# Merge and output projection of a two-block model in pairs of slabs, seven block products for eight, with the sums of weights on GpSimd

## The chip, the cores and the metric

The kernel runs on one core of one Trainium2 chip. The metric is the time of one execution on the device in microseconds (us), the median of the runs shown. All arithmetic spoken of here is fp32.

## What is computed

Two transformer-like blocks follow each other on a sequence of 512 tokens of width 1024. The first has differential attention, a state-space layer and a mixture of 32 experts. The second, of which the change touches the last part, is cut here to what matters:

```python
proj = h @ w_in                       # q, k, v, x_rnn, z_rnn, z_attn, g_r, g_a
y_rnn  = (hr * silu(z_rnn)) @ w_out_rnn
y_attn = (o * silu(z_attn)) @ w_out_attn
merged = sigmoid(g_r + b_r) * y_rnn + sigmoid(g_a + b_a) * y_attn
x = x + gate * (merged @ w_o)
return rms_norm(x, g_final)
```

g_r and g_a are two 1024x1024 products of h, y_rnn and y_attn one each of the gated recurrent output (`rnn_out`) and the gated attention output (`attn_out`), and the last one of `merged`: five products of 1024x1024 weights with 1024x512 activations.

## The kernel before

Every engine has a program of its own, and the programs meet at semaphores: the order on each engine is written out by hand. Activations are kept transposed, features on the 128 partitions and the 512 tokens along the free dimension, as tiles [128, 8, 512] (`h_t`, `rnn_out`, `attn_out`, `merged`, `x_t`). A weight matrix is cut into slabs: slab i holds the weights of 128 output features, [128, 8 k-tiles, 128]. One slab takes eight matmuls of 512 columns, added up in one PSUM bank. In the trace each fp32 matmul stands as two MATMUL records, and each record has its weight load (LDWEIGHTS) beside it.

The heads. Before the part in question, a loop over eight heads (`HEADS2`) runs, on TensorE, five slabs of a head (`turn_slab`, L1089: q, k, x_rnn, z_rnn, z_attn), the scores (L1116), the gates of the recurrence (L1119), the transposes of the softmax (L1124) and the product with v (L1137). ScalarE copies and squashes (L1504 to L1525; the transposed softmax is copied by L1274). VectorE rotates (L2116 to L2118), convolves (L2123, L2125), normalizes the softmax (L2139), does the recurrence (L2144 to L2152; the last of these counts `rnn gated`) and makes `attn_out` (L2157, counts `head gated`). GpSimd has nothing to do here.

The merge. In the last head the slot in which the next head's first slab would run is filled by `merge_slab(0, 0)`, after a wait for the first of four ScalarE copies. Then come the other 31 slabs (L1096), for i in 0..7 the four kinds g_r, o_r, g_a, o_a in PSUM banks 0 to 3. ScalarE makes the sigmoids from banks 0 and 2 (L1534), VectorE multiplies them with banks 1 and 3 (L2164) and adds the two into `merged` (L2166).

The output. Eight slabs of w_o (L1159) go into banks 4 to 7. VectorE adds each, times the gate, to x (L2169), ScalarE squares it (L1537), VectorE adds squares up (L2175), TensorE sums them over the partitions (`square_sum`, L805), ScalarE takes the root (L1539), and after a reciprocal (L2177) and four transposes (L1168) VectorE scales the output (L2181), which SyncE stores.

Loads. SyncE loads the merge slabs (512 KB each) into ring slots 5 to 8 and the w_o slabs into slots 0 to 3, each after a wait for the slab before it in its slot; turn slabs are in slots 0 to 4.

Of the kernel before, what the change touches and what calls it, by code (L numbers as in the profile page):

```python
# [11 lines left out]
ACT = mybir.ActivationFunctionType  # L12
# [73 lines left out]
MASKED = -1e30  # L86
PI = float(np.pi)
# [23 lines left out]
def program(nc, io):  # L111


    with ExitStack() as ctx:
# [182 lines left out]
        sig_r, sig_a = work[:, 0, :], work[:, 1, :]  # L297
# [26 lines left out]
        def sync_engine():  # L324
# [154 lines left out]
            for s in range(4):  # L479
                load_slab("merge", 5 + s, s)  # L480
# [13 lines left out]
            for s in range(4):  # L494
                if s < 2:
                    swap_halves(HEADS2 - 1, s)
                sp.wait_ge(sem("turn slabs used"), 5 * (HEADS2 - 1) + s + 1)
                load_slab("o", s, s)
            for i in range(1, KT):
                for s in range(4):  # L500
                    sp.wait_ge(sem("merge slabs used"), 4 * (i - 1) + s + 1)
                    load_slab("merge", 5 + s, 4 * i + s)
            for s in range(4):
                sp.wait_ge(sem("o slabs used"), s + 1)
                load_slab("o", s, 4 + s)
# [8 lines left out]
        def tensor_engine():  # L514
# [76 lines left out]
            pe.wait_ge(sem("ready for idle products"), 1)  # L591
# [4 lines left out]
            pe.wait_ge(sem("c_act"), 1)  # L596
# [47 lines left out]
            def s5_output(q):  # L644

                pe.wait_ge(sem("s5 states"), q + 1)
                if q:
                    pe.wait_ge(sem("s5 y read"), q)
                else:
                    pe.wait_ge(sem("s5 direct kept"), 1)  # L650
# [12 lines left out]
            def scores_of(i):  # L663
                q_h, k_h = proj[:, 4 + i, :], proj[:, 8 + i, :]
                pe.wait_ge(sem("pair kept"), kept[("slab", 5 + 3 * i)])
                if i:
                    pe.wait_ge(sem("p turned kept"), 4 * i)
                    pe.wait_ge(sem("masked"), 8 * i)
                else:
                    pe.wait_ge(sem("s5 direct kept"), 1)  # L670
                    pe.wait_ge(sem("s5 sums kept"), 8)
# [420 lines left out]
            def merge_slab(i, s):  # L1092

                pe.wait_ge(sem(f"slot {5 + s} loaded"), 16 * (i + 1) + (32 if s == 3 else 16 * 2 * (9 - ROWS_TO)))
# [5 lines left out]
            pe.wait_ge(sem("second tables loaded"), 32)  # L1100
            for i in range(HEADS2):
# [39 lines left out]
            pe.wait_ge(sem("rnn gated"), 8)  # L1141
            for i in range(KT):
                for s in range(4):
                    if (i, s) == (0, 0):
                        continue
                    if (i, s) == (0, 3):
                        pe.wait_ge(sem("head gated"), 8)
                    if i:
                        pe.wait_ge(sem("merge gate sig" if s % 2 == 0 else "merge gated"), 2 * (i - 1) + s // 2 + 1)
                    merge_slab(i, s)  # L1150
            for i in range(2):
                for s in range(4):
                    pe.wait_ge(sem(f"slot {s} loaded"), 16 * (15 + i))
                    if i:
                        pe.wait_ge(sem("x mixed"), 8 + s + 1)
                    for k in range(KT):
                        if (i, s) == (0, 0):
                            pe.wait_ge(sem("merged"), k + 1)
                        mm = pe.matmul(psum[:, 4 + s, :], ring[:, s, k, :], merged[:, k, :], start=(k == 0), stop=(k == KT - 1))  # L1159
                    mm.then_inc(sem("o slabs used"), 1)  # L1160

            pe.wait_ge(sem("squares added"), 12)
            square_sum(0, True, False)
            pe.wait_ge(sem("norm squares"), 24)
            square_sum(7, False, True).then_inc(sem("norm sum"), 1)
# [6 lines left out]
        def scalar_engine():  # L1172
# [133 lines left out]
            act.activation(flat[:, 4096:4608], psum[:, 4, :], ACT.Copy).then_inc(sem("s5 direct kept"), 1)  # L1306
# [162 lines left out]
            act.dma_start(pos_i, io["positions"]).then_inc(sem("second tables loaded"), 16)  # L1469
            act.dma_start(arena[:, low:low + 2048], io["rnn_gates"]).then_inc(sem("second tables loaded"), 16)  # L1470
# [23 lines left out]
            for i in range(HEADS2):  # L1494
# [22 lines left out]
                act.activation(tanh_g, r_g, ACT.Tanh, scale=all_par[:, 7, i:i + 1]).then_inc(sem("tanh made"), 1)  # L1517
                act.wait_ge(sem("tanh made"), i + 1)
# [9 lines left out]
            act.wait_ge(sem("head gated"), 8)  # L1528
            for i in range(KT):
                for n in range(2):  # L1530
                    act.wait_ge(sem("merge slabs used"), 4 * i + 2 * n + 1)
                    if i:
                        act.wait_ge(sem("merged"), i)
                    act.activation((sig_r, sig_a)[n], psum[:, 2 * n, :], ACT.Sigmoid, bias=gates_par[:, n, i:i + 1]).then_inc(sem("merge gate sig"), 1)  # L1534
            for k in range(KT):
                act.wait_ge(sem("x mixed"), 8 + k + 1)
                act.activation(h_t[:, k, :], x_t[:, k, :], ACT.Square).then_inc(sem("norm squares"), 1)  # L1537
            act.wait_ge(sem("norm sum"), 3)
            act.activation(last_std, psum[:, 1, 0:TT], ACT.Sqrt, bias=const("eps"), scale=1.0 / D).then_inc(sem("norm root"), 1)  # L1539


        def vector_engine():
# [11 lines left out]
            dve.memset(proj[:, 0, 0:2 * P], 0.0).then_inc(sem("ready for idle products"), 1)  # L1554
# [538 lines left out]
            dve.wait_ge(sem("second tables loaded"), 32)  # L2093
# [19 lines left out]
            for i in range(HEADS2):  # L2113
# [27 lines left out]
                dve.wait_ge(sem("a made"), i + 1)  # L2141
# [18 lines left out]
            for i in range(KT):  # L2160
                for n, sig in enumerate((sig_r, sig_a)):
                    dve.wait_ge(sem("merge slabs used"), 4 * i + 2 * n + 2)
                    dve.wait_ge(sem("merge gate sig"), 2 * i + n + 1)
                    dve.tensor_tensor(sig, sig, psum[:, 2 * n + 1, :], ALU.mult).then_inc(sem("merge gated"), 1)  # L2164
                dve.wait_ge(sem("merge gated"), 2 * i + 2)
                dve.tensor_tensor(merged[:, i, :], sig_r, sig_a, ALU.add).then_inc(sem("merged"), 1)  # L2166
            for k in range(KT):
                dve.wait_ge(sem("o slabs used"), k + 1)
                dve.scalar_tensor_tensor(x_t[:, k, :], psum[:, 4 + k % 4, :], mods[:, 64 + k:65 + k], x_t[:, k, :], ALU.mult, ALU.add).then_inc(sem("x mixed"), 1)  # L2169

                for n in {2: (1,), 3: (2,), 4: (3,), 5: (4,), 6: (5, 6)}.get(k, ()):
                    dve.wait_ge(sem("norm squares"), 16 + n + 1)
                    if n > 1:
                        dve.wait_ge(sem("squares added"), 6 + n - 1)
                    dve.tensor_tensor(h_t[:, 0, :], h_t[:, 0, :], h_t[:, n, :], ALU.add).then_inc(sem("squares added"), 1)  # L2175
# [3 lines left out]
            dve.wait_ge(sem("x mixed"), 16)  # L2179
# [4 lines left out]
        def gpsimd_engine():  # L2184
# [36 lines left out]
            for n in range(TT * TOPK):  # L2221
                pool.indirect_dma_start(out=parts[:, n, :], out_offset=None, in_=y_rows, in_offset=bass.IndirectOffsetOnAxis(ap=slot_i[:, n:n + 1], axis=0)
                                        ).then_inc(sem(f"parts {n // TOPK} gathered" if n >= TOPK else f"first parts {n} gathered"), 16)

# [87 lines left out]
def layout(a):  # L2312
# [23 lines left out]
    for part, (bb, cc) in enumerate(((a["ssm_b_re"], a["ssm_c_re"]), (a["ssm_b_im"], a["ssm_c_im"]))):  # L2336
# [23 lines left out]
        "merge_slabs": np.stack([g_r, o_r, g_a, o_a], 1).reshape(4 * KT, P, D),  # L2360
        "v_slabs": v, "o_slabs": o_o,
# [21 lines left out]
```

## Time and profile before

| | us |
|---|---|
| median of 3 runs | 2064.86 |
| lowest and highest run | 2064.61, 2068.92 |
| span of the profiled execution, first to last instruction | 2063.5 |

The profiled execution's own time is not listed apart; what it has beside the span is taken as the difference to the median, 1.4 us. In the profile PE is TensorE's matmuls, PEld its weight loads, DVE VectorE, ACT ScalarE, POOL GpSimd, SP SyncE. A row of a timeline has the start, the duration, the engine, the line, the operation with what it writes and reads, the count of merged instructions, and in brackets the idle time before it with what ended that. Since matmuls are pipelined and their ends are modelled, a stretch of PE is best read from the start of one row to the start of the next.

### The profile page before, as it was taken

The page shows a single profiled execution, that of the slowest core. Times are in us where ns is not written, and L with a number is a line of the kernel's source. Part 1 is how long each engine was busy: PE and PEld are TensorE (multiplying, and loading weights), DVE is VectorE, ACT ScalarE, POOL GpSimd, SP SyncE. Part 2 cuts the span into 40 slices and gives each one's busy share as a digit, 9 for nine tenths or more (in the row PEclk, how much of TensorE's full clock was granted, in tenths as well). Part 3 has the DMA queues.
Part 4 walks back from the last instruction along what each step waited for, and adds up shares of the span by engine and source line. Part 5 has one row for each costly group of instructions (what it writes and reads, how often), then busy time and mean ns, then how long its engine had stood idle before and what let it go on. Part 6 is the DMA issues. An engine that isn't in the chain of part 4 may idle for free.

```text
span 2063.5 us, 35675 instructions
## 1 busy us (share of the span) xinstructions
PE 1999.2 (97%) x15505; PEld 894.2 (43%) x15505; DVE 660.3 (32%) x1287; ACT 404.5 (20%) x837; POOL 52.8 (3%) x54
## 2 busy tenths in 40 slices
PE   8999998999999999999999999889999999999998
PEld 4455543334434434344333343455444444444443
DVE  5979864111111112121111121153434453300002
ACT  3224412111101101011011010112333533300001
POOL 0000000000000000000000000030000000000000
PEclk9999999999999999999999999989999999999999
DMA  8474788999899999999999999870312221122211
GB/s 328 142 289 182 304 289 343 420 419 361 327 421 419 420 420 419 419 420 420 420 419 419 418 418 420 343 265 15 111 65 74 64 65 65 53 80 74 80 33 69
DMA packets 109166, 553.77 MB, mean 268 GB/s; under 512 B 14864, under 2 KB 26128, under 8 KB 59216
## 3 DMA queue, kind: packets, MB, share of 16 engines
q1 hardware_dynamic: 87232, 517.23, 62.5%
q10 hardware_dynamic: 14720, 17.43, 2.5%
q0 software_dynamic: 7056, 16.79, 2.2%
q8 instruction: 125, 2.05, 0.4%
q14 instruction: 33, 0.27, 0.0%
HBM read 532.91 MB, written 26.35 MB: 271 GB/s over the span
## 4 chain that ended last, share of the span: by engine, by line
PE 69%; DMA 13%; SPq 13%; DVE 2%; issue 1%; ACT 1%; POOL 0%; ACTq 0%; POOLq 0%; DVEq 0%
PE psum L904 16%; PE psum L1089 13%; SPq L435 12%; PE psum L1096 11%; DMA arena<-in_w 7%; PE psum L912 7%; PE psum L575 7%; DMA ring<-in_w 3%; PE psum L1047 3%; PE psum L1159 3%; DMA arena<-in_mod_slabs 1%; PE psum L1137 1%; PE psum L1116 1%; PE psum L897 1%; PE psum L884 1%
## 5 line engine op out<-in xcount | busy, mean ns | idle before, releaser
L904 PE MATMUL psum<-arena,ring 128*32 128x512 f32 x4096 | 452.1, 595 | 12.4 <-DMA arena<-in_w 11.8
L1089 PE MATMUL psum<-h_t,ring 128*128 128x512 f32 x640 | 278.6, 593 | 0.2 <-ACT arena L1462 0.2
L904 PEld LDWEIGHTS psum<-arena,ring 128*32 128x32 f32 x4096 | 134.0, 110 | 310.8 <-issue 308.2
L912 PE MATMUL psum<-arena,h_t 128*32 128x256 f32 x3840 | 217.8, 380 | 4.0 <-DMA arena<-in_w 3.1
L1988 DVE TENSOR_SCALAR h_t<-psum 128x512 f32<-128x512 f32 (+2 forms) x33 | 27.9, 845 | 577.2 <-PE psum L904 577.2
L1390 ACT ACTIVATE ring<-psum,mods,gain 128x64 f32<-128x64 f32 (+2 forms) x264 | 85.6, 428 | 613.0 <-PE psum L884 613.0
L1089 PEld LDWEIGHTS psum<-h_t,ring 128*128 128x128 f32 x640 | 120.6, 190 | 146.2 <-issue 145.7
L912 PEld LDWEIGHTS psum<-arena,h_t 128*32 128x32 f32 x3840 | 121.0, 110 | 100.4 <-issue 18.7
L904 PE MATMUL psum<-ring 128*32 128x512 f32 x1344 | 148.8, 593 | 5.5 <-DMA ring<-in_w 5.4
L575 PE MATMUL psum<-h_t,ring 128*128 128x512 f32 x256 | 117.1, 613 | 2.6 <-ACT h_t L1210 2.6
L1096 PE MATMUL psum<-h_t,ring 128*128 128x512 f32 x256 | 112.6, 593 | 1.4 <-ACT work L1274 1.4
L1096 PE MATMUL psum<-arena,ring 128*128 128x512 f32 x256 | 112.5, 593 | 0.0
L912 PE MATMUL psum<-ring,h_t 128*32 128x256 f32 x1600 | 90.5, 380 | 3.2 <-DMA ring<-in_w 3.2
L904 PEld LDWEIGHTS psum<-ring 128*32 128x32 f32 x1344 | 44.4, 110 | 103.5 <-issue 103.5
L2002 DVE COPY h_t<-psum 128x512 f32<-128x512 f32 (+2 forms) x33 | 27.9, 845 | 154.9 <-PE psum L920 154.9
L575 PEld LDWEIGHTS psum<-h_t,ring 128*128 128x128 f32 x256 | 48.8, 196 | 63.7 <-issue 62.8
L1096 PEld LDWEIGHTS psum<-h_t,ring 128*128 128x128 f32 x256 | 48.6, 190 | 62.3 <-issue 60.7
L1096 PEld LDWEIGHTS psum<-arena,ring 128*128 128x128 f32 x256 | 48.6, 190 | 60.7 <-issue 60.7
L2164 DVE TENSOR_TENSOR work<-work,psum 128x512 f32<-128x512 f32 x16 | 11.0, 689 | 196.7 <-PE psum L1096 196.7
L1398 ACT ACTIVATE work<-psum 128x512 f32<-128x512 f32 (+2 forms) x33 | 23.8, 720 | 239.4 <-PE psum L912 239.4
L912 PEld LDWEIGHTS psum<-ring,h_t 128*32 128x32 f32 x1600 | 50.0, 110 | 42.9 <-issue 6.9
L2190 POOL DMA_INDIRECT ring<-h_rows,row_i x33 | 35.6, 1080 | 1143.5 <-PE psum L884 836.7
(440 smaller groups left out, 1748.9 us busy)
## 6 DMA issues: line engine op xcount, KB each, us to landing
arena<-in_w SPq DMA_DIRECT2D x288, 1024.0 KB, 27.8
ring<-in_w SPq DMA_DIRECT2D x96, 1024.0 KB, 29.2
ring<-in_dot_slabs SPq DMA_DIRECT2D x40, 512.0 KB, 5.6
ring<-in_turn_slabs SPq DMA_DIRECT2D x40, 512.0 KB, 3.4
ring<-in_merge_slabs SPq DMA_DIRECT2D x32, 512.0 KB, 3.3
ring<-in_mod_slabs SPq DMA_DIRECT2D x6, 2048.0 KB, 10.8
ring<-in_proj_slabs SPq DMA_DIRECT2D x24, 512.0 KB, 4.1
y_rows<-arena SPq DMA_DIRECT2D x3, 3584.0 KB, 25.4
```

What stands on the lines that cost most here:

```text
L435: sp.dma_start(slot[s], source).then_inc(sem(f"weights {s} loaded"), 16)
L575: mm = pe.matmul(bank, ring[:, n % 4, k, :], src[:, k, :], start=(k == 0), stop=(k == KT - 1))
L904: mm = pe.matmul(psum[32 * j:32 * j + 32, g, :], x_e[:, c * tokens + g * TG:c * tokens + g * TG + TG], slot[s][:, j * S:(j + 1) * S], star ...
L912: mm = pe.matmul(psum[32 * j:32 * j + 32, 6 + g // 2, (g % 2) * 256:(g % 2) * 256 + 256], h_e[:, g * 256 + half * P + 32 * c:g * 256 + hal ...
L1047: mm = pe.matmul(psum[:, 4 + i, :], h_t[:, k, t * P:(t + 1) * P], ring[:, 4 * i + 4:4 * i + 8, k, :], start=(k == 0), stop=(k == KT - 1))
L1089: mm = pe.matmul(psum[:, bank, :], ring[:, s, k, :], h_t[:, k, :], start=(k == 0), stop=(k == KT - 1))
L1096: mm = pe.matmul(psum[:, s, :], ring[:, 5 + s, k, :], (h_t, rnn_out, h_t, attn_out)[s][:, k, :], start=(k == 0), stop=(k == KT - 1))
L1159: mm = pe.matmul(psum[:, 4 + s, :], ring[:, s, k, :], merged[:, k, :], start=(k == 0), stop=(k == KT - 1))
L1390: act.activation(x_e[:, k * tokens:(k + 1) * tokens], psum[:, 4 + k // 4, (k % 4) * tokens:(k % 4 + 1) * tokens], ACT.Identity, bias=mods[ ...
L1988: dve.tensor_scalar(gate, psum[:, 0:groups, 0:256], LIMIT, None, ALU.min).then_inc(sem("gate clipped"), 1)
L2002: dve.tensor_copy(h_e[:, 0:256 * groups], src[:, 0:256 * groups]).then_inc(sem("h_e kept"), 1)
L2190: pool.indirect_dma_start(out=x_g[n][0:rows, :], out_offset=None, in_=h_rows, in_offset=bass.IndirectOffsetOnAxis(ap=index, axis=0), bound ...
```

## The change

The 32 merge slabs and 8 output slabs are taken in pairs, in the order of `MERGE_PAIRS`: for j in 0..3 the pairs (g_r, g_a, o_r, o_a), then four pairs of w_o; 20 in all. A pair is a product of a 256x1024 matrix with 1024x512 activations. Weights are halved along the output features (`first`, `second` slab) and along the input features (k-tiles 0:4 and 4:8), activations along the input features and the tokens (`front`, `back`, 256 each). Seven block products of four matmuls with 256 columns then take the place of eight, in Winograd's arrangement of Strassen's scheme, with eight sums of operands and seven of results:

- GpSimd makes four sums of activations for each source (`moving_sums`: h, rnn_out, attn_out with four operations of [128, 4, 256], merged in two parts) and four sums of weights for each pair (`slab_sums`: four operations of [128, 4, 128], one of them in place). `slab_sums(n)` waits for the load of pair n and for the end of pair n-2, whose buffers it takes. In GpSimd's program the sums of rnn_out and attn_out stand behind `slab_sums(1)` and ahead of `slab_sums(2)`.
- ScalarE copies the first product (`keep_p1`), makes sigmoids in quarters of the pair, and squares in quarters.
- VectorE makes `u2`, `u4` and three blocks (256 columns each) for a pair, then the gating (`y gated`, `merged`) and, for the last two slabs of merged, the sums of activations (`last merged sums`).
- The five additions of squares move from VectorE to GpSimd.
- SyncE loads 20 pairs of 1 MB into ring slots 5-6, 7-8 and 0-1, pair n after the end of pair n-3.
- Some semaphores are merged into others, their waits renumbered.

TensorE, cut to its core:

```diff
-            def merge_slab(i, s):
-                pe.wait_ge(sem(f"slot {5 + s} loaded"), ...)
-                for k in range(KT):
-                    mm = pe.matmul(psum[:, s, :], ring[:, 5 + s, k, :], (h_t, rnn_out, h_t, attn_out)[s][:, k, :], start=(k == 0), stop=(k == KT - 1))
-                mm.then_inc(sem("merge slabs used"), 1)
+            def product(out, stationary, moving, start=False):
+                for k in range(4):
+                    mm = pe.matmul(out, stationary[:, k, :], moving[:, k, :], start=(start and k == 0), stop=(k == 3), skip_group_check=True)
+                mm.then_inc(sem("products"), 1)
+
+            def pair_begun(n):
...
+                product(block_x, first[:, 0:4, :], moving[:, 0:4, front], True)
+                pe.wait_ge(sem("slab sums"), 4 * n + 2)
+                if n:
+                    pe.wait_ge(sem("pair steps"), 5 * (n - 1) + U2)
+                if (kind, j) == ("o", 0):
+                    pe.wait_ge(sem("moving sums"), 16)
+                    pe.wait_ge(sem("last merged sums"), 2)
+                product(block_x2, mixed[:, 1, :, :], t2, True)
+                pe.wait_ge(sem("x bank kept"), P1_KEPT(n))
+                if (kind, j) == ("o", 0):
+                    pe.wait_ge(sem("merged"), 8)
+                product(block_x, first[:, 4:8, :], moving[:, 4:8, front])
+                if n:
+                    pe.wait_ge(sem("pair steps"), 5 * (n - 1) + U4)
+                else:
+                    pe.wait_ge(sem("p turned kept"), 16 + 4 * HEADS2)
+                product(block_v, mixed[:, 0, :, :], t1, True)
+
+            def pair_ended(n):
...
+                product(block_q, second[:, 0:4, :], t3, True)
+                pe.wait_ge(sem("slab sums"), 4 * n + 4)
+                if n:
+                    pe.wait_ge(sem("pair steps"), 5 * (n - 1) + BLOCK_12)
+                product(block_w, mixed[:, 2, :, :], moving[:, 4:8, back], True)
+                pe.wait_ge(sem("pair steps"), 5 * n + BLOCK_22)
+                if (kind, j) == ("o", 0):
+                    pe.wait_ge(sem("last merged sums"), 3)
+                product(block_q, second[:, 4:8, :], t4)
...
-                    pe.wait_ge(sem("p turned kept"), 16 + 4 * i + 1)
-                    merge_slab(0, 0)
+                    pe.wait_ge(sem("rnn gate sig"), 2 * i + 2)
+                    pair_begun(0)
```

GpSimd and VectorE:

```diff
+            def slab_sums(n):
+                at = PAIR_AT[n % 3]
+                first, second, (s1, s2, s4) = ring[:, at, :, :], ring[:, at + 1, :, :], (sums_of[n % 2][:, a, :, :] for a in range(3))
+                pool.wait_ge(sem(f"slot {PAIR_AT[n % 3]} loaded"), PAIR_LOADED[n % 3] + 16 * (n // 3 + 1))
+                if n >= 2:
+                    pool.wait_ge(sem("products"), 7 * (n - 2) + 7)
+                else:
+                    pool.wait_ge(sem("turn slabs used"), 5 * (HEADS2 - 1) + 4 + n)
+                pool.tensor_tensor(s1, second[:, 0:4, :], second[:, 4:8, :], ALU.add).then_inc(sem("slab sums"), 1)
+                pool.wait_ge(sem("slab sums"), 4 * n + 1)
+                pool.tensor_tensor(s2, s1, first[:, 0:4, :], ALU.subtract).then_inc(sem("slab sums"), 1)
+                pool.tensor_tensor(second[:, 0:4, :], first[:, 0:4, :], second[:, 0:4, :], ALU.subtract).then_inc(sem("slab sums"), 1)
+                pool.wait_ge(sem("slab sums"), 4 * n + 2)
+                pool.tensor_tensor(s4, first[:, 4:8, :], s2, ALU.subtract).then_inc(sem("slab sums"), 1)
+
+            moving_sums(0, h_t, h_sums)
+            slab_sums(0)
+            slab_sums(1)
+            pool.wait_ge(sem("rnn gated"), 8)
+            moving_sums(4, rnn_out, rnn_sums)
+            pool.wait_ge(sem("head gated"), 8)
+            moving_sums(8, attn_out, attn_sums)
+            for n in range(2, 16):
+                slab_sums(n)
...
+            def u2_of(n):
+                dve.wait_ge(sem("products"), 7 * n + 2)
+                dve.wait_ge(sem("x bank kept"), P1_KEPT(n))
+                dve.tensor_tensor(u2, block_x2, p1_kept, ALU.add).then_inc(sem("pair steps"), 1)
+
+            def u4_of(n):
+                dve.wait_ge(sem("products"), 7 * n + 4)
+                dve.wait_ge(sem("pair steps"), 5 * n + U2)
+                dve.tensor_tensor(u4, block_v, u2, ALU.add).then_inc(sem("pair steps"), 1)
+                dve.wait_ge(sem("pair steps"), 5 * n + U4)
+
+            def block(n, products, out, bank, u):
+                dve.wait_ge(sem("products"), 7 * n + products)
+                dve.tensor_tensor(out, bank, u, ALU.add).then_inc(sem("pair steps"), 1)
```

## Rows read from the trace of the kernel before

**Rows 1.** The page's head: span, busy time of each engine, clock granted to TensorE.

```profile
span 2063.5 us, 35675 instructions
...
PE 1999.2 (97%) x15505; PEld 894.2 (43%) x15505; DVE 660.3 (32%) x1287; ACT 404.5 (20%) x837; POOL 52.8 (3%) x54
...
PEclk9999999999999999999999999989999999999999
```

**Rows 2.** Windows: the merge, the output slabs, the tail (busy us of each engine).

```profile
1783.40:1996.30 212.90, 212.90 (x499) 94.38 (x498) 15.86 (x23) 10.99 (x16) 0.00 (x0) 1.00 0.20 68
1996.30:2051.20 54.90, 54.90 (x129) 24.32 (x128) 10.32 (x15) 4.42 (x7) 0.00 (x0) 1.00 0.11 39
2051.20:2063.50 12.30, 3.13 (x21) 2.54 (x19) 6.28 (x10) 2.18 (x3) 0.00 (x0) 0.61 0.46 171
```

**Rows 3.** Timeline of PE: end of the last head, first and last merge slabs.

```profile
1760.90 2.32 PE L1116 MATMUL psum<-arena 128*128 128x128 f32 x8
1763.06 1.88 PE L1119 MATMUL psum<-arena 128*128 128x512 f32 x4
...
1771.65 1.26 PE L1124 MATMUL psum<-consts,work 128*128 128x128 f32 x10
1774.28 7.13 PE L1096 MATMUL psum<-h_t,ring 128*128 128x512 f32 x16 [1.38 <-ACT work L1274]
1781.25 2.32 PE L1137 MATMUL psum<-work,arena 128*128 128x512 f32 x8
1783.40 7.03 PE L1096 MATMUL psum<-arena,ring 128*128 128x512 f32 x16
1790.28 7.03 PE L1096 MATMUL psum<-h_t,ring 128*128 128x512 f32 x16
...
1989.41 7.03 PE L1096 MATMUL psum<-arena,ring 128*128 128x512 f32 x16
1996.27 55.10 PE L1159 MATMUL psum<-arena,ring 128*128 128x512 f32 x128
```

**Rows 4.** Timeline of PEld in the tail: eight weight loads for one-column matmuls.

```profile
2052.87 0.97 PEld L805 LDWEIGHTS psum<-consts,h_t 128*128 128x128 f32 x8 [0.81 <-ACT h_t L1537]
```

**Rows 5.** Timeline of ACT at the end of the last head.

```profile
1773.65 1.40 ACT L1274 ACTIVATE work<-psum 128x512 f32<-128x512 f32 x4
1775.06 1.28 ACT L1525 ACT_TABLE_LOAD   x1
1776.36 0.60 ACT L1525 ACTIVATE arena<-psum 128x512 f32<-128x512 f32 x1
```

**Rows 6.** Groups by line and form: DVE and ACT with 256 columns (mean ns).

```profile
L1774 DVE CUSTOM_DVE_ANT_0 work<-psum,consts 128x256 f32<-128x256 f32 x8 | 3.4, 420 | 0.0
L1274 ACT ACTIVATE work<-psum 128x256 f32<-128x256 f32 x8 | 3.1, 383 | 0.0
```

**Rows 7.** Timeline of DVE at the end of the last head.

```profile
1773.78 0.69 DVE L2144 TENSOR_TENSOR arena<-arena 128x512 f32<-128x512 f32 x1 [5.66 <-ACT arena L1520]
...
1779.39 0.69 DVE L2152 TENSOR_TENSOR arena<-arena 128x512 f32<-128x512 f32 x1
...
1783.68 0.69 DVE L2157 TENSOR_TENSOR arena<-psum,arena 128x512 f32<-128x512 f32 x1 [3.00 <-PE psum L1137]
```

**Rows 8.** Groups by line and form of POOL: its one operation on much data.

```profile
L2186 POOL MEMSET arena<- 128x1024 f32 x1 | 1.0, 952 | 48.8 <-PE psum L551 48.8
```

**Rows 9.** The chain that ended last, from the last output slab on.

```profile
1996.44 54.95 PE psum L1159 x128
...
2051.41 0.76 DVE x_t L2169
...
2052.19 0.63 ACT h_t L1537
```

**Rows 10.** DMA issues: KB each, median us from issue to landing.

```profile
ring<-in_merge_slabs SPq DMA_DIRECT2D x32, 512.0 KB, 3.3
ring<-in_mod_slabs SPq DMA_DIRECT2D x6, 2048.0 KB, 10.8
```

More of the change, by code:

```diff
@@ L86 @@
 MASKED = -1e30
+HALF = S // 2
+MERGE_PAIRS = [(kind, j) for j in range(KT // 2) for kind in ("g_r", "g_a", "o_r", "o_a")] + [("o", j) for j in range(KT // 2)]
 PI = float(np.pi)
@@ L493, in sync_engine @@
                     load_slab("turn", s, 5 * i + s)
[L494 to L505, printed above, removed]
+            for s in range(2):
+                swap_halves(HEADS2 - 1, s)
+            sp.wait_ge(sem("turn slabs used"), 5 * (HEADS2 - 1) + 2)
+            load_pair(2)
+            for n in range(3, len(MERGE_PAIRS)):
+                sp.wait_ge(sem("products"), 7 * (n - 3) + 7)
+                load_pair(n)
             for k in range(KT):
@@ L588, in keep_on @@
                     pe.matmul(psum[:, bank, :], identity, dilated, start=True, stop=True, skip_group_check=True)
-            pe.wait_ge(sem("ready for idle products"), 1)
+            pe.wait_ge(sem("c_act"), 1)
             for _ in range(14):
@@ L595, in tensor_engine @@
             rms_sum(0, h_t)
[L596 removed]
+            pe.wait_ge(sem("c_act"), 2)
             mod_row(0, 0)
@@ L1099, in tensor_engine @@
             pe.wait_ge(sem("v rows kept"), 8)
-            pe.wait_ge(sem("second tables loaded"), 32)
+            pe.wait_ge(sem("late tables loaded"), 64)
             for i in range(HEADS2):
@@ L1138, in tensor_engine, with token_squares @@
                 mm.then_inc(sem("head out"), 1)
[L1141 to L1165, printed above, removed]
+            pair_ended(0)
+            for n in range(1, len(MERGE_PAIRS)):
+                pair_begun(n)
+                pair_ended(n)
+            def token_squares(k, tiles, first=False, last=False):
+                for t in tiles:
+                    mm = pe.matmul(psum[:, 6, t:t + 1], h_t[:, k, t * P:(t + 1) * P], ones[:, 0:1], start=(first and t == 0), stop=last, skip_group_check=True)
+                return mm
+            pe.wait_ge(sem("squares added"), 6 + 5)
+            token_squares(0, range(TT), first=True)
+            pe.wait_ge(sem("norm squares"), 16 + 4 * 4 - 1)
+            token_squares(6, range(TT))
+            token_squares(7, (2, 3), last=True)
+            pe.wait_ge(sem("norm squares"), 16 + 4 * 4)
+            token_squares(7, (0, 1), last=True).then_inc(sem("norm sum"), 1)
             pe.wait_ge(sem("tile scale"), TT + 2)
@@ L1525, in scalar_engine @@
                 act.activation(za_s, psum[:, 6, :], ACT.Sigmoid).then_inc(sem("z_attn sig"), 1)
[L1528 to L1534, printed above, removed]
@@ L1551, in scaled @@
                     dve.scalar_tensor_tensor(h_t[:, k, :], x_t[:, k, :], gain[:, k:k + 1], rstd, ALU.mult, ALU.mult).then_inc(sem("h scaled"), 1)
-            dve.memset(proj[:, 0, 0:2 * P], 0.0).then_inc(sem("ready for idle products"), 1)
+            dve.memset(proj[:, 0, 0:2 * P], 0.0).then_inc(sem("c_act"), 1)
             dve.wait_ge(sem("sines"), 1)
@@ L2157, in vector_engine @@
                 dve.tensor_tensor(attn_out[:, i, :], psum[:, 7, :], za_s, ALU.mult).then_inc(sem("head gated"), 1)
[L2160 to L2166, printed above, removed]
@@ new lines, in mixed @@
+            def mixed(k, part, y):
+                dve.scalar_tensor_tensor(x_t[:, k, part], y, mods[:, 64 + k:65 + k], x_t[:, k, part], ALU.mult, ALU.add).then_inc(sem("x mixed"), 1)
+            for n, (kind, j) in enumerate(MERGE_PAIRS):
+                if kind != "o":
+                    continue
+                u2_of(n)
+                dve.wait_ge(sem("products"), 7 * n + 3)
+                dve.scalar_tensor_tensor(x_t[:, 2 * j, front], block_x, mods[:, 64 + 2 * j:65 + 2 * j], x_t[:, 2 * j, front], ALU.mult, ALU.add).then_inc(sem("x mixed"), 1)
+                u4_of(n)
+                for step_made, products, i, part, bank, u in ((BLOCK_22, 5, 1, back, block_q, u4), (BLOCK_12, 6, 0, back, block_w, u4), (BLOCK_21, 7, 1, front, block_q, u2)):
+                    block(n, products, y_pair[:, i, part], bank, u)
+                    dve.wait_ge(sem("pair steps"), 5 * n + step_made)
+                    mixed(2 * j + i, part, y_pair[:, i, part])
@@ new lines, in gpsimd_engine @@
+            pool.wait_ge(sem("h ready"), 8 + KT * TT)
+            pool.wait_ge(sem("v product"), 8)
+            moving_sums(0, h_t, h_sums)
[7 more added lines that the diff above has]
+                slab_sums(n)
+            t1, t2, t3, t4 = h_sums
+            pool.wait_ge(sem("products"), 7 * 14)
@@ new lines, in gpsimd_engine @@
+            pool.tensor_tensor(t4[:, 0:2, :], merged[:, 4:6, front], t2[:, 0:2, :], ALU.subtract).then_inc(sem("moving sums"), 1)
+            for n in range(16, len(MERGE_PAIRS)):
+                slab_sums(n)
+            for n, (k, squares_made) in enumerate(((1, 4), (2, 8), (3, 8), (4, 12), (5, 12))):
+                pool.wait_ge(sem("norm squares"), 16 + squares_made)
+                if n:
+                    pool.wait_ge(sem("squares added"), 6 + n)
+                pool.tensor_tensor(h_t[:, 0, :], h_t[:, 0, :], h_t[:, k, :], ALU.add).then_inc(sem("squares added"), 1)
```

167 lines of the change are left out of this document (139 added, 28 removed).

## The prediction

> **What bounds the kernel now.** I read the page's head first: PE is busy 97% of 2063.5 us at full clock, every other engine a third or less [rows 1]. The windows then show the stretch that is changed: 212.9 us of merge and 54.9 us of output slabs, in which PE is busy all the time, DVE at most 19%, ACT 8%, POOL not at all [rows 2]. So here PE's own work is the time, and what shortens it counts in full as long as nothing new makes PE wait. The timeline of PE gives the unit: slabs start at 1783.40, 1790.28, and the last at 1989.41, the output slabs at 1996.27: (1996.27 - 1783.40) / 31 = 6.867 us for a slab, and a first output matmul that waited for nothing [rows 3]. A pair of slabs costs 13.73 us. The chain that ended last goes from the last slab through DVE and ACT to the end, so a gain on PE moves the whole tail forward [rows 9].
>
> **The change, part by part.**
>
> 1. *Seven products for eight.* A pair becomes 7 x 4 = 28 matmuls of 256 columns, 56 records. A record of 512 columns takes 6.867 / 16 = 0.4292 us. To cost one of 256 I need the fixed part. L1137 and L1116 each run eight records of 512, 384, 256 and 128 columns (two each, 2560 in all) and take 1783.40 - 1781.25 = 2.15 and 1763.06 - 1760.90 = 2.16 us [rows 3]. With a + b x columns, the first gives b = 0.836 ns, a = 1.4 ns, the second b = 0.829 and a = 4.7. A record of 256 columns is then 0.2153 to 0.2170 us; I take 0.216. A pair costs 56 x 0.216 = 12.10 us and saves 1.63 us (1.58 to 1.67). Weight loads could set the pace now that a record is half as long, but eight of them with matmuls of one column took 0.97 us, 0.12 each, well under 0.216 [rows 4].
>
> 2. *The waits between products.* There are now 140 seams on PE with up to four waits each instead of 40 with two. L1137 ends in records of 128 columns, and the slab behind it, with two waits ahead of it (its load and `rnn gated`), starts without a gap in the 2.15 us above [rows 3]. I take a met wait at nothing; the cover is the record that runs meanwhile. Below nothing it can't go, since the waits are added. The other end I leave to a rival.
>
> 3. *The first pair.* `merge_slab(0, 0)` waited 1.38 us for ACT's copy; `pair_begun(0)` waits for gates that were ready earlier and starts right behind the transposes, at 1771.65 + 10 x 0.109 = 1772.74. P1 and P2 take 1.73 each, to 1776.2. P3 waits for `keep_p1`, which stands on ACT behind the sigmoid that ends at 1776.96 [rows 5] and takes 0.38 [rows 6]: P3 starts at 1777.4, P4 ends at 1780.85, the product with v at 1783.0, against 1783.40. P5 to P7 end at 1788.2. DVE is in time for P7's wait (P7 would start at 1786.5): `attn_out` from 1783.3 to 1784.0 [rows 7], then u2, u4 and the first block at 0.42 each [rows 6], the last behind P5: 1785.4. Before, two slabs ended at 1790.28. Gain 2.1 us. The other 19 pairs give 19 x 1.63 = 31.0.
>
> 4. *DVE and ACT inside a pair.* Five steps of 0.42 and, for o pairs, two to four of 0.69 [rows 6, 7] make at most 4.9 us of DVE in 12.1; ACT has at most five of about 0.4 to 0.5. Each PE wait on them has a product (1.73 us) or more between the work and its use: keeping P1 (0.38) beside P2, block 22 (0.42) beside P6. Hidden, at nothing. If a step came 1.3 us late, it would show as that excess times 20.
>
> 5. *Entering the output product.* Before, no gap [rows 3]. Now, with T the end of pair 15, DVE has from T - 1.5 on one block (0.42), the gating, merged, and two sums of 0.72 each: ready at T + 1.8; P2 of pair 16 wants it at T + 1.73. The front half follows at T + 3.75, for P3 at T + 3.5. Loss 0.3 us.
>
> 6. *Loads.* 1 MB per pair, issued when pair n-3 ends, so 12.1 us before GpSimd may begin on it. 512 KB landed in 3.3 us, 2048 KB in 10.8 [rows 10]: 1 MB within 11, hidden. SP's other work, the swaps of the last head, keeps its place ahead of load 2.
>
> 7. *GpSimd's sums.* The trace has no such operation. The nearest POOL row is a memset of 1024 columns, 0.952 us, so 0.48 us for 512, with one stream [rows 8]; DVE's addition of 512 takes 0.69 [rows 7]. A sum has three streams, two in and one out. Taking the memset's rate for each gives t = 3 x 0.48 = 1.43 us per 512 columns. I take that; ends are 0.48 (one stream) and twice 1.43, 2.9. Four per pair are 5.7 us against 12.1, hidden in the steady state. The tight place is pair 2: behind `slab_sums(1)` stand the sums of rnn_out and attn_out, and then S1 and S2 of pair 2. `rnn gated` comes at 1780.1 [rows 7]; from there on the queue holds 8 operations of 1024 columns and 2 of 512, 18 t. PE wants S2 after P1 of pair 2, at 1788.2 + 12.1 + 1.73 = 1802.0. The slack is 21.9 us, used up at t = 1.22. With 1.43 it is 18 x 1.43 = 25.7 plus some 0.3 of handing over: PE stands 4.1 us. Behind it GpSimd catches up, since 5.7 is less than 12.1. The sums of h (8 t) come in the first head, seven heads before their use; those of merged begin at the end of pair 13 and have 25 us for 9 t.
> The Trainium skill, "GPSIMD Engine Reference", section 3.1, states 4497 ns for an addition of 2048 columns. That would be t = 1.12 (an estimate from that page), with no stall at pair 2 and a time 4.1 us lower than my sum; no row here shows it.
>
> 8. *Tail.* Instead of L2169 and the square (0.76 and 0.63 us [rows 9]) three steps of 0.42 with 256 columns follow the last product: 0.1 us less. The additions of squares on GpSimd end a pair earlier than needed.
>
> Sum against the profiled execution: 2063.5 - 2.1 - 31.0 + 0.3 + 4.1 - 0.1 = 2034.7 us. The median of the runs lies 1.4 us over that span, so I expect 2036.0.
>
> **The rivals.**
>
> *All hidden.* t is under 1.22, so pair 2 does not wait: 4.1 less, 2031.9. For it: the memset's rate leaves room for 2.5 streams in 1.22 us. Against: three streams.
>
> *GpSimd and VectorE hold each other up.* If the two can't read two operands each at once, whoever comes second waits a whole operation. It bites where both have such work. In the last head, DVE's recurrence (eight operations from 1773.78 on [rows 7]) meets `slab_sums(1)`, begun at 1771.8: the third DVE operation starts at 1778.9 and not 1775.2, so `rnn gated`, and pair 2 with it, comes 3.7 us later. At the entry of the output product `slab_sums(17)` begins at T, and between DVE's five operations stand three or four of 1.43: merged is ready at T + 8.9 for 3.75, 5.2 lost. Together 8.9: 2045; with t = 1.2 the same working gives 2.8 + 4.2, on top of no stall otherwise: 2039. Before, POOL ran nothing in these stretches [rows 2], so the rows say nothing for or against. The Trainium skill, "SBUF — State Buffer", section "Who interferes with whom", says that a VectorE instruction with two SBUF inputs and a GpSimd one that reads SBUF share a read interface and block each other for the whole instruction; by that rule this rival holds. No row here shows it.
>
> *The seams on PE cost.* A wait costs 0.1 us at each of 140 products: 14 us, 2050. Against it, the seam behind L1137.
>
> *Slower: GpSimd becomes the bound.* With t over 3.03, four sums outlast the 12.1 us of a pair. With t = 3.5: 18 x 3.5 - 21.9 = 41 at pair 2, and 17 x (14 - 12.1) = 32 behind it, less the 33 gained: 2105. It decides from t = 3.05, where pair 2 alone eats 33 us. It takes six memsets' time for one sum; little speaks for that.
>
> That the scheme doesn't shorten PE (matmuls of 256 columns at the price of 512) is excluded by the 2.15 us of L1137.
>
> **How the numbers follow.** Forecast, a stall of 2 to 7 us at pair 2, 2033 to 2039: 0.40. All hidden: 0.22, near 2031.9. Holding up, 2039 to 2046: 0.22. Seams, 2040 to 2050: 0.07. t from 1.7 to 3, 2041 to 2064: 0.06. Slower: 0.03. The range 2031.0 to 2047.0 holds the first three and part of the others. 0.2% is about 4 us, what a measurement of this kernel tells from no change; all cases but t near 3 and the slower one lie beyond: faster 0.95, same 0.02, slower 0.03.
>
> **What would show it.** In the new timeline, PE's P1 of consecutive pairs 12.1 us apart; records of 256 columns 0.216 apart; one gap of some 4 us ahead of P2 of pair 2, released by POOL; POOL sums of 512 columns near 1.43 us; DVE's recurrence in the last head still 0.69 each with 0.03 between (holding up shows as gaps or long operations beside POOL's); a gap under 0.5 us around P2 and P3 of pair 16. Gaps at most products would make the seams right; P2 waiting for POOL in every pair, GpSimd as bound.

## The result and the profile after

The changed kernel takes 2040.13 us (median of 4 runs, 2039.04 to 2041.46) against 2065.30 of the kernel before in the same runs: a ratio of 0.9868, 95% interval 0.9854 to 0.9882. That is 25.2 us less; 28.8 were forecast. The profiled run took 2039.04 us, 1.3 us more than its span of 2037.7.

The page's head, as in [rows 1], and its groups of the new products and sums:

```profile
span 2037.7 us, 37038 instructions
...
PE 1973.6 (97%) x15993; PEld 991.7 (49%) x15993; DVE 718.6 (35%) x1392; ACT 421.9 (21%) x889; POOL 199.3 (10%) x155
...
L1117 PE MATMUL psum<-arena,ring 128*128 128x256 f32 x544 | 120.5, 380 | 1.6 <-POOL ring L2386 1.4
...
L2384 POOL TENSOR_TENSOR ring<-ring 128x512 f32<-128x512 f32 x20 | 25.3, 1267 | 416.7 <-PE psum L1112 314.9
```

PE is 25.6 us less busy, POOL 146 us more. The waits of PE at the new products (L1117) are a short list (the view of the waits: who waits, for whom, total, times, longest):

```profile
PE psum L1117 <- DVE ring L2297: 2.0, 1, 2.0
PE psum L1117 <- ACT work L1604: 1.8, 1, 1.8
PE psum L1117 <- POOL ring L2386: 1.4, 1, 1.4
```

Three single waits, none that comes back with each pair. The timeline of PE shows where they stand (as [rows 3]):

```profile
1772.58 1.26 PE L1203 MATMUL psum<-consts,work 128*128 128x128 f32 x10
1773.67 1.89 PE L1117 MATMUL psum<-h_t,ring 128*128 128x256 f32 x8
1775.40 1.89 PE L1117 MATMUL psum<-ring 128*128 128x256 f32 x8
1779.04 1.99 PE L1117 MATMUL psum<-h_t,ring 128*128 128x256 f32 x8 [1.76 <-ACT work L1604]
...
1789.94 1.89 PE L1117 MATMUL psum<-h_t,ring 128*128 128x256 f32 x8
1791.66 1.89 PE L1117 MATMUL psum<-ring 128*128 128x256 f32 x8
...
1802.03 1.89 PE L1117 MATMUL psum<-arena,ring 128*128 128x256 f32 x8
1805.33 22.71 PE L1117 MATMUL psum<-arena,ring 128*128 128x256 f32 x104 [1.42 <-POOL ring L2386]
...
1976.86 3.22 PE L1117 MATMUL psum<-ring 128*128 128x256 f32 x8 [2.04 <-DVE ring L2297]
1980.21 2.27 PE L1117 MATMUL psum<-arena,ring 128*128 128x256 f32 x8
1982.32 3.62 PE L1117 MATMUL psum<-ring 128*128 128x256 f32 x16
...
2025.48 2.73 PE L1228 MATMUL psum<-consts,h_t 128*128 128x1 f32 x24
```

The first product of pair 1 starts at 1789.94, that of pair 2 at 1802.03: a pair takes 12.09 us. A product of eight records takes 1.727 us from start to start (1791.66 - 1789.94), 0.216 a record, and seven of them make the whole 12.09: nothing is left for the waits between them.

The part ahead of the last head isn't touched but for small edits, and from one profiled run to another it ends up to 8.5 us apart (the transposes start between 1769.3 and 1777.8). So I read every profile from the start of the last head's transposes (L1203; L1124 before) to the end of the span. Before, that is 2063.5 - 1771.65 = 291.85 us, after 2037.7 - 1772.58 = 265.1: 26.7 us gained, and 0.9 lost ahead of it. That 0.9 lies inside the 8.5 us by which this point moves, and I did not look further.

| us, from the transposes on | forecast | measured |
|---|---|---|
| pair 0 | 2.1 less | 1.3 less (1789.94 - 1772.58 against 1790.28 - 1771.65) |
| 19 pairs | 31.0 less | 31.2 less (19 x (13.73 - 12.09)) |
| gap at pair 2 | 4.1 more | 1.6 more (second product at 1805.33, due at 1791.66 + 12.09) |
| entry of pair 16 | 0.3 more | 4.3 more (fourth product at 1982.32, due 1805.33 + 3.45 + 14 x 12.09 = 1978.04) |
| tail | 0.1 less | 0.1 less (2037.7 - 2025.48 against 2063.5 - 2051.21) |
| sum | 28.8 less | 26.7 less |

The large term is right to 1%. The small ones are off in both directions, and the timelines of DVE and POOL say why. First the recurrence in the last head (as [rows 7]) and what POOL does beside it:

```profile
1775.53 1.76 DVE L2239 TENSOR_TENSOR arena<-arena 128x512 f32<-128x512 f32 x1 [5.66 <-ACT arena L1592]
1777.32 1.63 DVE L2240 SCALAR_TENSOR_TENSOR arena<-arena 128x512 f32<-128x512 f32 x1
1778.99 0.69 DVE L2241 TENSOR_TENSOR arena<-arena 128x512 f32<-128x512 f32 x1
...
1783.16 0.69 DVE L2247 TENSOR_TENSOR arena<-arena 128x512 f32<-128x512 f32 x1
```

```profile
1774.24 1.28 POOL L2386 TENSOR_TENSOR ring<-ring 128x512 f32<-128x512 f32 x1
1775.47 1.28 POOL L2387 TENSOR_TENSOR ring<-ring 128x512 f32<-128x512 f32 x1
1776.70 1.71 POOL L2389 TENSOR_TENSOR ring<-ring 128x512 f32<-128x512 f32 x1
1783.93 2.36 POOL L2369 TENSOR_TENSOR arena<-arena 128x1024 f32<-128x1024 f32 x1 [5.52 <-DVE arena L2247]
```

The second operation of the recurrence in the kernel before, with the first one in [rows 7]:

```profile
1774.50 0.69 DVE L2145 SCALAR_TENSOR_TENSOR arena<-arena 128x512 f32<-128x512 f32 x1
```

As long as POOL works, the first two DVE operations take 1.76 and 1.63 us where they took 0.69, and those after it is done take 0.69; POOL's last one takes 1.71 instead of 1.28. The recurrence lasts 8.3 us from the first start to the end of L2247 where it lasted 6.3. The same at the entry of pair 16, DVE and POOL:

```profile
1972.58 0.69 DVE L2290 TENSOR_TENSOR arena<-work 128x512 f32<-128x512 f32 x1
1973.31 1.74 DVE L2296 TENSOR_TENSOR ring<-arena,ring 128x512 f32<-128x512 f32 x1
1974.97 1.75 DVE L2297 TENSOR_TENSOR ring<-arena 128x512 f32<-128x512 f32 x1
1976.64 0.41 DVE L2268 TENSOR_TENSOR arena<-psum,work 128x256 f32<-128x256 f32 x1
1977.08 1.31 DVE L2287 TENSOR_TENSOR work<-work,arena 128x512 f32<-128x512 f32 x1
1978.42 1.64 DVE L2290 TENSOR_TENSOR arena<-work 128x512 f32<-128x512 f32 x1
```

```profile
1973.23 1.26 POOL L2384 TENSOR_TENSOR ring<-ring 128x512 f32<-128x512 f32 x1 [6.69 <-PE psum L1117]
...
1977.80 1.71 POOL L2389 TENSOR_TENSOR ring<-ring 128x512 f32<-128x512 f32 x1
```

L2268, with one input in PSUM and one in SBUF, keeps its 0.41 us in the midst of it; four operations with both inputs in SBUF are held up (1.31 to 1.75 us for 0.69). The end of L2290 at 1980.06 is the earliest at which the third product can start.

### The profile page after: what moved, and what is told of

It is laid out like the page before. It is cut to its first block, busy times and chain, and to the rows that moved or that the text cites. A ratio compares the mean times of both kernels' runs of the same rounds, so it can differ in the third digit from the quotient of the medians.

```text
span 2037.7 us, 37038 instructions
## 1 busy us (share of the span) xinstructions
PE 1973.6 (97%) x15993; PEld 991.7 (49%) x15993; DVE 718.6 (35%) x1392; ACT 421.9 (21%) x889; POOL 199.3 (10%) x155
## 3 DMA queue, kind: packets, MB, share of 16 engines
q8 instruction: 129, 2.11, 0.4%
## 4 chain that ended last, share of the span: by engine, by line
PE 69%; SPq 14%; DMA 10%; DVE 3%; issue 1%; POOL 1%; ACT 1%; ACTq 0%; POOLq 0%; DVEq 0%
PE psum L927 17%; SPq L458 14%; PE psum L1112 13%; PE psum L1117 11%; PE psum L935 8%; PE psum L598 7%; DMA ring<-in_w 5%; DMA arena<-in_w 3%; PE psum L1070 3%; DMA arena<-in_mod_slabs 1%; PE psum L920 1%; PE psum L1195 1%; PE psum L1216 1%; PE psum L907 1%; PE psum L782 1%
## 5 line engine op out<-in xcount | busy, mean ns | idle before, releaser
L1112 PE MATMUL psum<-h_t,ring 128*128 128x512 f32 x640 | 278.6, 592 | 0.2 <-ACT arena L1534 0.2
L1112 PEld LDWEIGHTS psum<-h_t,ring 128*128 128x128 f32 x640 | 120.4, 190 | 146.4 <-issue 145.9
L1117 PE MATMUL psum<-arena,ring 128*128 128x256 f32 x544 | 120.5, 380 | 1.6 <-POOL ring L2386 1.4
L598 PE MATMUL psum<-h_t,ring 128*128 128x512 f32 x256 | 116.3, 609 | 2.6 <-ACT h_t L1282 2.6
L1117 PEld LDWEIGHTS psum<-arena,ring 128*128 128x128 f32 x544 | 103.4, 191 | 16.7 <-POOL ring L2386 1.8
L598 PEld LDWEIGHTS psum<-h_t,ring 128*128 128x128 f32 x256 | 48.4, 194 | 62.4 <-issue 61.3
L1117 PE MATMUL psum<-ring 128*128 128x256 f32 x288 | 67.6, 384 | 2.0 <-DVE ring L2297 2.0
L2384 POOL TENSOR_TENSOR ring<-ring 128x512 f32<-128x512 f32 x20 | 25.3, 1267 | 416.7 <-PE psum L1112 314.9
L1117 PEld LDWEIGHTS psum<-ring 128*128 128x128 f32 x288 | 55.2, 192 | 10.0 <-POOL ring L2386 2.4
```

Source lines behind the costliest of these rows:

```text
L598: mm = pe.matmul(bank, ring[:, n % 4, k, :], src[:, k, :], start=(k == 0), stop=(k == KT - 1))
L1112: mm = pe.matmul(psum[:, bank, :], ring[:, s, k, :], h_t[:, k, :], start=(k == 0), stop=(k == KT - 1))
L1117: mm = pe.matmul(out, stationary[:, k, :], moving[:, k, :], start=(start and k == 0), stop=(k == 3), skip_group_check=True)
L2384: pool.tensor_tensor(s1, second[:, 0:4, :], second[:, 4:8, :], ALU.add).then_inc(sem("slab sums"), 1)
```

## The experiments

Two theories. A: GpSimd and VectorE block each other where both read two operands from SBUF, and this is what lies behind the gap at pair 16, the late recurrence and part of the other two gaps. B: the gaps are the length of the chains on VectorE and of GpSimd's queue, and the slow operations only coincide with them.

The 95% intervals of the ratios of e2, e3 and e5 overlap that of the changed kernel (0.9854 to 0.9882, repeated 0.9842 to 0.9894). Their gains are therefore read from the profiles, one profiled execution each, over the stretch from the transposes on; there the changed kernel repeats to 0.1 us (e6).

**e1_small_sums.** GpSimd's sums are made on one column only, in `moving_sums`, `slab_sums` and the sums of merged.

```diff
+            def tiny(out, one, two, op):
+                return pool.tensor_tensor(out[:, 0, 0:1], one[:, 0, 0:1], two[:, 0, 0:1], op)
...
-                pool.tensor_tensor(s1, second[:, 0:4, :], second[:, 4:8, :], ALU.add).then_inc(sem("slab sums"), 1)
+                tiny(s1, second[:, 0:4, :], second[:, 4:8, :], ALU.add).then_inc(sem("slab sums"), 1)
```

> Every sum on GpSimd is done on one column only, with the same waits and counts, so GpSimd takes almost no time and the output is not the reference's (the sums of weights and activations are left out). Theory A (GpSimd and VectorE block each other when both read two operands from SBUF, and the stall at pair 2 is GpSimd's queue): the VectorE operations of the recurrence in the last head go back from 1.7 to 0.69 us, the 1.4 us gap ahead of the second product of pair 2 goes, and at the entry of pair 16 the 2.0 us gap and the slow matmuls behind it go: 5.1 us less than the changed kernel, near 2035. Theory B (the waits lie in the order of the work on VectorE and in PE's seams, GpSimd only happens to run beside it): the gap at pair 2 goes, 1.4 us less, the VectorE operations stay at 1.7 us and pair 16 keeps its gap. Both: the 1.8 us wait for ScalarE's copy in the last head stays.

Measured: 2033.16 us, ratio 0.9834 (0.9821 to 0.9847) to the kernel before. The recurrence runs at 0.69 again, the gaps at pairs 2 and 16 are gone, and from the transposes on it takes 258.8 us, 6.3 less than the changed kernel. The sums of weights and activations are left out in this kernel, so it is no candidate, only a measure. Its list of waits holds one of the three, and smaller than expected:

```profile
PE psum L1117 <- ACT work L1604: 0.9, 1, 0.9
```

That was a miss of both theories as I had put them (1.8 was expected to stay): part of this wait hangs on GpSimd too. The last run, e8, shows how.

**e2_hold_17.**

```diff
             for n in range(16, len(MERGE_PAIRS)):
+                if n == 17:
+                    pool.wait_ge(sem("last merged sums"), 3)
                 slab_sums(n)
```

> GpSimd waits with the sums of pair 17 until VectorE has made its last sums of merged, so that nothing runs on GpSimd beside VectorE's gating at the entry of pair 16. Theory A: VectorE's five operations there take 0.69 each again, PE's gap of 2.0 us shrinks to under 0.4, no half clock follows (1.6 us of it in the second product of pair 16 and 0.4 in the third), together 3.5 to 4 us less than the changed kernel: near 2036.5. Theory B: the gap stays as it is, since the chain on VectorE is what it is. The last head and pair 2 stay as in the changed kernel.

Measured: 2035.62 us, ratio 0.9851 (0.9837 to 0.9864). From the transposes on 261.1 us, 4.0 less than the changed kernel, all of it at pair 16. DVE and PE there:

```profile
1973.48 0.69 DVE L2296 TENSOR_TENSOR ring<-arena,ring 128x512 f32<-128x512 f32 x1
1974.09 0.69 DVE L2297 TENSOR_TENSOR ring<-arena 128x512 f32<-128x512 f32 x1
...
1975.87 0.69 DVE L2290 TENSOR_TENSOR arena<-work 128x512 f32<-128x512 f32 x1
```

```profile
1974.93 1.97 PE L1117 MATMUL psum<-ring 128*128 128x256 f32 x8
1976.73 1.95 PE L1117 MATMUL psum<-arena,ring 128*128 128x256 f32 x8
1978.51 3.62 PE L1117 MATMUL psum<-ring 128*128 128x256 f32 x16
```

The second product starts at 1974.93, the fourth 3.58 later, where 3.45 is the undisturbed spacing: with 0.1 us ahead of the second product some 0.2 us are left, near the 0.3 that the prediction gave this place. Theory B falls at pair 16; the chain on VectorE is short enough when nothing runs on GpSimd beside it.

**e3_apart.**

```diff
             slab_sums(0)
-            slab_sums(1)
             pool.wait_ge(sem("rnn gated"), 8)
+            slab_sums(1)
             moving_sums(4, rnn_out, rnn_sums)
+            slab_sums(2)
             pool.wait_ge(sem("head gated"), 8)
             moving_sums(8, attn_out, attn_sums)
-            for n in range(2, 16):
+            for n in range(3, 16):
                 slab_sums(n)
```

> GpSimd waits for the end of VectorE's recurrence in the last head before it makes the sums of pair 1, and makes the sums of pair 2 ahead of those of attn_out. Theory A: the recurrence's first two operations go from 1.76 and 1.63 to 0.69, so that it ends 2.0 us earlier, near 1781.2 against 1783.2; the gap of 1.4 us at pair 2 goes, none comes at pair 1 (its sum is needed at 1791.7 and ready near 1784) nor at pair 3; 1.4 us less than the changed kernel, near 2038.7, the gap at pair 16 stays. Theory B: the recurrence stays as long as it was.

Measured: 2035.74 us, ratio 0.9849 (0.9836 to 0.9863); from the transposes on 262.7, 2.4 less than the changed kernel. All six plain operations of the recurrence take 0.69 us and no gap stands at pairs 1 to 3. The gain is 1 us beyond the expectation; the last section says where it comes from.

**e5_order.** `slab_sums(1)` stays beside the recurrence.

```diff
             moving_sums(4, rnn_out, rnn_sums)
+            slab_sums(2)
             pool.wait_ge(sem("head gated"), 8)
             moving_sums(8, attn_out, attn_sums)
-            for n in range(2, 16):
+            for n in range(3, 16):
```

> Only the order of GpSimd's work is changed: the sums of pair 2 stand ahead of the sums of attn_out, the sums of pair 1 still run beside VectorE's recurrence. If the gap at pair 2 is the length of GpSimd's queue alone, it goes (1.6 us less than the changed kernel, near 2038.5), while the recurrence's two slow operations of 1.7 us stay: blocking there costs nothing once the queue has room. If the late recurrence reaches PE in another way (through attn_out or block 22 of pair 0), a gap shows in pair 0 or at pair 3.

Measured: 2034.40 us, ratio 0.9855 (0.9827 to 0.9883; its runs scatter from 2027.75 to 2039.92). From the transposes on 262.7, the same as e3_apart. The recurrence has its 1.74 and 1.63 us, the gap at pair 2 is gone and none has come for it. So a late recurrence costs nothing by itself; it cost 1.6 us because the queue ahead of pair 2 had no room to spare.

**e6_changed_again.** The changed kernel without an edit.

> The changed kernel once more, beside the other runs of this call: near 2040, with 1.8 us ahead of the third product, 1.4 at pair 2, 2.0 at pair 16 and a pair in 12.09 us. It tells how far the time of one kernel moves between calls; every theory expects the same.

Measured: 2037.47 us, ratio 0.9868 (0.9842 to 0.9894), the same ratio as at first. From the transposes on 265.2 (265.1 at first), with gaps of 1.8, 1.4 and 2.05 us. The two profiled spans differ by 1.5 us (2037.7 and 2036.2), all of it ahead of that stretch; the medians differ by 2.7.

**e4_ten_sums.** Each of the first two sums of weights four times.

```diff
+                for _ in range(3):
+                    step(pool, pool.tensor_tensor(s1, second[:, 0:4, :], second[:, 4:8, :], ALU.add), "more sums")
                 pool.tensor_tensor(s1, second[:, 0:4, :], second[:, 4:8, :], ALU.add).then_inc(sem("slab sums"), 1)
```

> The first two sums of weights of each pair are made four times each, ten operations in place of four. If GpSimd's work is hidden as long as it is shorter than a pair (both theories) its ten operations take about 12.9 us beside a pair of 12.1: PE waits some 0.8 us in each pair behind pair 2, 14 us in all, the queue ahead of pair 2 grows by some 12 us and the sums of merged put another 6 on the path ahead of pair 16: 2065 to 2075, no gain over the kernel before. If the sums were already in PE's way in every pair, it would be 20 x 7.9 = 158 us more.

Measured: 2084.71 us, ratio 1.0084 (1.0068 to 1.0099): slower than before, by more than expected, and far from 158 us. PE's waits from the second block on:

```profile
PE psum L1117 <- POOL ring L2390: 35.9, 15, 11.5
PE psum L1117 <- DVE work L2268: 3.7, 1, 3.7
PE psum L1117 <- ACT work L1604: 1.2, 1, 1.2
```

The 11.5 us are pair 2, as computed from the queue; 9.1 of the other 24.4 stand at pair 16, where 6 were expected. The expectation missed two things. The ten operations take 13.1 us a pair even where nothing holds them up (1853.43 to 1866.51), not 12.9: each added one waits for the one before, 1.35 us from start to start and not 1.23. Beside VectorE they take up to 14.7 (1838.75 to 1853.43, single ones 1.60 to 1.72 for 1.27). And VectorE's recurrence is now blocked eight times, so that attn_out and block 22 of pair 0 come late (3.7). The slower side is there once GpSimd's work outlasts the 12.09 us of a pair, here by 1 us and more; where exactly it begins no run shows.

**e7_all_mended.** e3_apart and e2_hold_17 together, and ScalarE's copy of the first product of pair 0 ahead of the last sigmoid:

```diff
                 keep_turned(4 + i + 1, pt2)
+                if i == HEADS2 - 1:
+                    act.wait_ge(sem("products"), 1)
+                    act.activation(p1_kept, block_x, ACT.Copy).then_inc(sem("x bank kept"), 1)
...
             for n, (kind, j) in enumerate(MERGE_PAIRS):
-                keep_p1(n)
+                if n:
+                    keep_p1(n)
```

> Four edits together: GpSimd's sums of pair 1 behind the recurrence, those of pair 2 ahead of attn_out's, those of pair 17 behind VectorE's last sums of merged, and ScalarE's copy of the first product of pair 0 ahead of the last sigmoid and its table load. Theory A: 1.6 at pair 2, 4.0 at pair 16 and 1.7 at the third product go: 7.3 less than the changed kernel of the same call, near 2032.8. If the product with v, now 1.7 us earlier, has to wait for something else in the last head, 5.6 less.

Measured: 2028.14 us (2027.96 to 2032.63), ratio 0.9829 (0.9803 to 0.9855), against 2037.47 (2035.84 to 2037.91) of the changed kernel run beside it: 9 us less, and no run of one reaches a run of the other. In the profiles, from the transposes on, it is 257.2 against 265.2, 8.0 us: 1.9 in pair 0, 1.6 at pair 2, 4.0 at pair 16, and 0.4 in the tail, which the last section speaks of. No product of L1117 waits; what is left of the list are 0.7 us in the tail and 0.2 in the first head. The product with v started earlier and found all it needed.

**e8_and_row_max.** As e7, and:

```diff
             moving_sums(0, h_t, h_sums)
+            pool.wait_ge(sem("row max"), HEADS1 + HEADS2)
             slab_sums(0)
```

> As the one before, and GpSimd's sums of pair 0 wait for the row maxima of the last head, so that VectorE's small scaling there (1.00 us in the changed kernel, 0.17 in the kernel before) isn't blocked. Theory A: it takes 0.17 us again and the chain through the exponentials to the copy comes 0.8 us earlier; PE gains at most what is left of a gap ahead of the third product (0.2 us or less), so the same time within 0.5 us; if the four scalings behind it are blocked in its place and end later than the transposes want them, 0.5 us more.

Measured: 2029.21 us, ratio 0.9831 (0.9805 to 0.9858), from the transposes on 257.4: no difference from e7. The small scaling in the kernel before, in e7, and in e8 with the reciprocal and the four scalings of the softmax behind it:

```profile
1764.10 0.17 DVE L2134 TENSOR_SCALAR small<-small 128x4 f32<-128x4 f32 x1
```

```profile
1766.54 1.00 DVE L2233 TENSOR_SCALAR small<-small 128x4 f32<-128x4 f32 x1
```

```profile
1763.83 0.17 DVE L2233 TENSOR_SCALAR small<-small 128x4 f32<-128x4 f32 x1
1766.36 0.18 DVE L2235 RECIPROCAL inverse<-small 128x4 f32<-128x4 f32 x1 [2.36 <-ACT work L1332]
1766.57 3.30 DVE L2238 TENSOR_SCALAR work<-work,inverse 128x128 f32<-128x128 f32 x4
```

This explains the miss of e1, where the scaling also took 0.17 us. In the changed kernel `slab_sums(0)` holds an operation on four numbers per partition for 0.8 us, and behind it come the exponentials, the gates and at last the copy for which the third product waits. Counted from the transposes, the first exponential and that copy both start 0.8 us earlier in e8 than in e7 (the copy 3.27 us behind their start and not 4.11). In e8 the four scalings of the softmax are held instead (3.30 us for 1.27), which hurts nobody, as TensorE wants them later.

Theory A as I had put it is too narrow here. These scalings read one tensor from SBUF, not two, and are held; the reciprocal at 1766.36, also with one input, ran beside a sum of GpSimd (1765.43 to 1766.70) in its usual 0.18 us. What sets the two apart no run here shows.

## Why the prediction came out as it did

The time lies in the stated range of 16 us, but 4.1 us above the 2036.0 that the sum gave; the large steps hold. *Point 1*, a record of 256 columns at 0.216 us from the mixed groups of the kernel before: measured 0.216. *Point 2*, a met wait costs nothing: seven products fill the pair to the hundredth of a microsecond, so the rival of the seams has no share. *Points 4, 6 and 8*: no wait on DVE or ACT in any pair but 0 and 16, loads of 1 MB landing in 4.8 us (median), a tail 0.1 us shorter.

*The step that failed* is the one where I took GpSimd's work as a neighbour that takes only its own time, and gave the likeliest case a seam at pair 16 of 0.3 us. It was 4.3, and e2 takes 4.0 of it away by moving GpSimd's work. This was the rival of engines that hold each other up; its place was right (both the recurrence and pair 16), its prices somewhat high: 3.7 us for the recurrence, measured 2.0, since POOL's sums are shorter and only two of the four were left when the recurrence began; 5.2 for pair 16, measured 4.0. The measured 2040 lies in that rival's interval (2039 to 2046), not in the forecast's (2033 to 2039); its variant with t = 1.2 gave 2039, and t was measured near that. I gave it 0.22 because no row of before could speak for it.

The Trainium skill's rule ("SBUF — State Buffer", "Who interferes with whom": two SBUF inputs on VectorE and a reading GpSimd operation exclude each other for the whole instruction) agrees with the traces: 1.76 us where 0.69 stood, 0.69 again as soon as POOL is done, and 0.41 as ever for the operation with an input in PSUM.

*Point 7* was mis-sized the other way. t was taken as 1.43 us from three times the memset's rate; it is 1.27, and 1.23 from start to start (2.36 and 2.31 for 1024 columns). The queue of 18 t from the end of `rnn gated` at 1783.85 to the second sum of pair 2 at 1805.29 took 21.4 us, inside the 21.9 of slack; the gap of 1.6 came because its start was 2.0 us late against TensorE. (Counted from the transposes it was 2.8 us late, 2.0 from the recurrence and 0.8 from the small scaling; but pair 0, held by the same scaling, was 0.8 late as well.) e3 and e5 both remove it, the one with the recurrence free and the other with it still blocked: the order of the queue decides.
From the two sizes follow 2.1 ns a column and 0.15 us fixed, an estimate of 4.5 us for 2048 columns: the 4497 ns of the Trainium skill, "GPSIMD Engine Reference", section 3.1, agree, but scaled down to 512 without the fixed part they gave 1.12, which is too low.

*Point 3*: pair 0 gained 1.3 and not 2.1, since ScalarE's copy came later: the third product waited 1.8 us where I had 1.2. e1, e7 and e8 show the cause, the small scaling held for 0.8 us.

So two errors of opposite sign partly cancel. t too long made the forecast 4.1 us too late, since with the true t and a recurrence on time pair 2 would not have waited at all. Blocking left out made it 6.4 too early: 4.0 at pair 16, 1.6 at pair 2, 0.8 at pair 0. That the sum of the stretch came within 2.1 us is luck.

## What to carry to other kernels

Work moved to an idle engine isn't free because that engine is idle: ask which operations of its neighbour it holds up, and look for the places where these are on the path. Here all pairs but three hid it. Pairs 16, 2 and 0, where TensorE waits on a chain at once, paid 4.3, 1.6 and 0.8 us; holding GpSimd back at the first and reordering its queue at the second gave back 4.0 and 1.6. Where work is queued in order on a helper, count the queue from its latest start to its first use, not only its load against the period.

## What was not expected

After the gap of 2.04 us at pair 16 TensorE's granted clock fell. The windows of the changed kernel from 1976.86 and from 1980.20 on (busy us of the engines, then the granted clock):

```profile
1976.86:1980.20 3.34, 3.21 (x8) 2.11 (x9) 3.23 (x4) 0.00 (x0) 2.65 (x2) 0.58 0.11 44
1980.20:1984.00 3.80, 3.79 (x16) 3.35 (x17) 1.40 (x3) 0.42 (x1) 0.00 (x0) 0.92 0.00 0
```

A granted clock of 0.58 over the first window means that the second product ran mostly at 1.2 instead of 2.4 GHz: 3.22 us for 1.89. It also happened in the repetition (e6, 0.57), not in e3 and e5 with a gap of the same length (PE in e3, where the clock stayed at 1.00):

```profile
1980.41 1.97 PE L1117 MATMUL psum<-ring 128*128 128x256 f32 x8 [2.05 <-DVE ring L2297]
1983.75 1.97 PE L1117 MATMUL psum<-arena,ring 128*128 128x256 f32 x8 [1.38 <-DVE arena L2290]
```

There the product is quick and the third one waits 1.38 us for merged, so it begins 3.34 us after the second, against 3.35 at the low clock. The low clock thus cost only what it took from the third product: 2.11 to the fourth in place of 1.81, 0.3 us. The transposes in the tail show the other share: 0.65 us in e3 and e5 at a granted clock of 1.00, 1.11 in the changed kernel at 0.50 (0.75 in e7, 1.11 in e8). These two make up 0.8 of the 1 us by which e3 and e5 beat their expectations, and the gap at pair 2, 1.6 us and not the 1.4 of the list, makes up the rest. Why two of the four gaps of 2 us lowered the clock and two did not stays open.
